# Two passes of 256 token columns instead of one pass of 512 in the matrix multiplications of a hybrid encoder trunk

## The reference, cut to what matters

```python
def swiglu(x, w_gate, w_up, w_down):
    return (jax.nn.silu(x @ w_gate) * (x @ w_up)) @ w_down

def hybrid_mixer(u, w_in, ...):
    proj = u @ w_in
    qa, ka, va, us, qc, kc, vc, fc = jnp.split(proj, IN_SPLITS, axis=-1)
    ya = swa_sink_attention(qa, ka, va, ...)     # sliding window
    yb = s5_mixer(us, ...)                       # state space scan
    yc = fox_attention(qc, kc, vc, fc, ...)      # forgetting attention
    y = jnp.concatenate([rms_norm(ya, ga), rms_norm(yb, gb), rms_norm(yc, gc)], axis=-1)
    return y @ w_out

for l in range(DEPTH):                           # DEPTH = 2
    h = h + 0.5 * rms_norm(swiglu(rms_norm(h, g[0]), ffn1_gate[l], ffn1_up[l], ffn1_down[l]), g[1])
    h = h + rms_norm(hybrid_mixer(rms_norm(h, g[2]), w_in[l], ..., w_out[l], cos, sin), g[3])
    h = h + 0.5 * rms_norm(swiglu(rms_norm(h, g[4]), ffn2_gate[l], ffn2_up[l], ffn2_down[l]), g[5])
```

## Time and profile before

| | us |
|---|---|
| median of the two runs | 2172.43 |
| the two runs | 2170.24 and 2174.62 |
| span of the profiled execution, first to last instruction | 2170.5 |
| PE busy in it | 2018.1 (93%) |
| DVE busy | 1206.8 (56%) |
| ACT busy | 875.6 (40%) |

### The profile page before, as it was taken

How to read it: one execution, slowest core, us unless ns; L and a number is a source line. 1 busy time by engine, 2 the same in 40 slices (tenths; PEclk the granted TensorE clock), 3 DMA queues, 4 the chain that set the end, 5 groups by cost and what they waited for, 6 DMA issues and landing times.

```text
span 2170.5 us, 27124 instructions
## 1 busy us (share of the span) xinstructions
PE 2018.1 (93%) x8694; PEld 1553.9 (72%) x8694; DVE 1206.8 (56%) x1645; ACT 875.6 (40%) x1380; POOL 436.5 (20%) x609
## 2 busy tenths in 40 slices
PE   5999999897998999999979999998889989999996
PEld 4888878564556688888758888885545667888885
DVE  3666643479864655553255555236887655555423
ACT  4444422343453544442144444224334635444322
POOL 4666765435400000000000000004552000000000
PEclk8999999999999999999989999999989999999998
DMA  4444344232102233333213333323210123333320
GB/s 113 121 126 121 116 129 125 77 88 69 39 20 69 68 97 97 97 113 93 66 58 99 97 96 105 107 69 98 78 59 20 40 59 88 96 96 100 116 84 39
DMA packets 330105, 187.03 MB, mean 86 GB/s; under 512 B 6440, under 2 KB 324304, under 8 KB 330032
## 3 DMA queue, kind: packets, MB, share of 16 engines
q1 hardware_dynamic: 323696, 167.08, 26.6%
q0 software_dynamic: 6336, 19.05, 2.8%
HBM read 175.59 MB, written 10.49 MB: 86 GB/s over the span
## 4 chain that ended last, share of the span: by engine, by line
PE 75%; DVE 11%; issue 7%; ACT 5%; DVEq 0%; POOL 0%; DMA 0%; SPq 0%; ACTq 0%; POOLq 0%
PE ps L375 16%; PE ps L377 15%; PE ps L376 15%; PE ps L451 7%; PE ps L452 7%; PE ps L453 7%; PE ps L413 2%; DVE rot L1289 1%; DVE wl L1089 1%; PE ps L528 1%; ACT wh L712 1%; PE ps L596 1%; DVE prob L1340 1%; PE ps L516 1%; DVE gst L1302 1%
## 5 line engine op out<-in xcount | busy, mean ns | idle before, releaser
L375 PE MATMUL ps<-xh,wh 128*128 128x512 f32 x1776 | 714.6, 402 | 66.3 <-DVE xl L1099 48.2
L376 PE MATMUL ps<-xl,wh 128*128 128x512 f32 x1776 | 697.7, 393 | 0.0
L377 PE MATMUL ps<-xh,wl 128*128 128x512 f32 x1776 | 697.5, 393 | 0.0
L1089 DVE TENSOR_TENSOR wl<-raw,wh 128x1024 fp32r<-128x1024 f32 (+1 forms) x288 | 387.0, 1344 | 527.0 <-ACT wh L712 523.2
L712 ACT ACTIVATE wh<-raw 128x1024 fp32r<-128x1024 f32 (+1 forms) x288 | 322.1, 1119 | 461.6 <-PE ps L453 317.7
L375 PEld LDWEIGHTS ps<-xh,wh 128*128 128x128 f32 x1776 | 336.9, 190 | 182.9 <-DVE wl L1089 45.6
L377 PEld LDWEIGHTS ps<-xh,wl 128*128 128x128 f32 x1776 | 337.1, 190 | 72.3
L376 PEld LDWEIGHTS ps<-xl,wh 128*128 128x128 f32 x1776 | 337.8, 190 | 69.6 <-issue 3.1
L451 PE MATMUL ps<-Hh,wh 128*128 128x512 f32 x704 | 276.5, 393 | 2.5 <-DVE wl L1089 2.4
L452 PE MATMUL ps<-Hl,wh 128*128 128x512 f32 x704 | 277.2, 394 | 0.0
L453 PE MATMUL ps<-Hh,wl 128*128 128x512 f32 x704 | 273.4, 388 | 0.0
(11 more groups left out here) (208 smaller groups left out, 2009.6 us busy)
## 6 DMA issues: line engine op xcount, KB each, us to landing
raw<-in_ffn_gate SPq DMA_DIRECT2D x88, 512.0 KB, 3.7
raw<-in_ffn_up SPq DMA_DIRECT2D x88, 512.0 KB, 3.8
raw<-in_ffn_down SPq DMA_DIRECT2D x64, 704.0 KB, 4.4
raw<-in_w_in SPq DMA_DIRECT2D x28, 512.0 KB, 3.8
ssm_tables<-tabw POOLq DMA_DIRECT2D x32, 256.0 KB, 2.5
tab<-ssm_tables POOLq DMA_DIRECT2D x16, 512.0 KB, 3.7
raw<-in_w_out SPq DMA_DIRECT2D x16, 512.0 KB, 3.8
yF<-in_x SPq DMA_DIRECT2D x1, 2048.0 KB, 9.5
```

The costliest lines, as they stand in the source:

```text
L375: pe.matmul(bank, wh[:, slot, kw, :], xh[:, kx, :], start=first, stop=False)
L376: pe.matmul(bank, wh[:, slot, kw, :], xl[:, kx, :], start=False, stop=False)
L377: return pe.matmul(bank, wl[:, slot, kw, :], xh[:, kx, :], start=False, stop=last)
L1089: V.tensor_tensor(wl[:, slot2, 0:nk, :], raw[:, slot4, 0:nk, :], wh[:, slot2, 0:nk, :].bitcast(F32), ALU.subtract).then_inc(w_split, 1)
```

## The change

`unit_x` no longer calls `three` but a new helper `three_of`, which takes a slice of the tokens. It goes through the unit's 8 blocks for tokens 0 to 255, and then again for tokens 256 to 511. `first_two`, `project_half` and the down projection keep their 512 columns. The matmul that clears the marks of the bank is still only the first one of the unit; the two halves write different columns of the bank. Waits and signals are where they were: one wait on `w_split` ahead of the unit, and one increment of `unit_done` behind it.

```diff
+            def three_of(out_, slot, kw, kx, tok, first, last):
+
+                pe.matmul(out_, wh[:, slot, kw, :], xh[:, kx, tok], start=first, stop=False, skip_group_check=True)
+                pe.matmul(out_, wh[:, slot, kw, :], xl[:, kx, tok], start=False, stop=False, skip_group_check=True)
+                return pe.matmul(out_, wl[:, slot, kw, :], xh[:, kx, tok], start=False, stop=last, skip_group_check=True)
+
             def unit_x(n, slot, bank, k0=0, nk=KD):
 
                 pe.wait_ge(w_split, n + RAW_SLOTS + 1)
-                for k in range(nk):
-                    mm = three(bank, slot, k, k0 + k, k0 + k == 0, k0 + k == KD - 1)
+                for half in range(2):
+                    tok = slice(half * (SEQ // 2), (half + 1) * (SEQ // 2))
+                    for k in range(nk):
+                        mm = three_of(bank[:, tok], slot, k, k0 + k, tok, half == 0 and k0 + k == 0, k0 + k == KD - 1)
                 mm.then_inc(unit_done, 1)
```

## The result

The changed kernel takes 2228.97 us (two runs, 2228.85 and 2229.09) against 2172.43 us, a ratio of 1.026 with an interval of 1.0241 to 1.028: 56.5 us slower. The profiled execution is the run of 2228.85 us, its span 2227.3 us.

A forecast was written before the change was run, and what follows sets the result against it. TensorE's matmul starts were taken to bound the changed loops; 4656 × 2.3 ns = 10.7 us, with loads free, took the span from 2170.5 to 2181.2, plus 1.9 to the median: 2183 us, range 2158 to 2240.

The forecast's parts named there:

- What bounds the kernel: In the gate and up loop, how often TensorE can start a matmul sets the end; one every 226 ns.
- How many: In `unit_x`, 4656 of 8694 matmuls become 9312 of 256 columns, adding 4656 weight loads and 4656 starts.
- The weight loads: In the cut units, 256 columns hide a full weight load, only 2.3 ns stay fixed; the loads cost nothing.
- The third rival: In the cut units, fp32r loads can't run under 256 columns: +220 ns a pair, +1026 us, 3199 us; chance 0.04.
- rival 2: In the cut units, the extra time disappears for narrow streams: 109 ns each, −40 us, 2132 us; chance 0.07.
- rival 4: In the cut units, 256-column fp32r streams run at fp32's rate: +205 ns a pair, +955 us, 3127 us; chance 0.05.
- The other 11 ns: In `unit_x` matmuls, 11.1 ns go with the columns: 114.5 ns per half, +2.3 ns a pair, +10.7 us.
- rival 1: At every start in `unit_x`, 11.1 ns are paid once per matmul or load: +63 us, 2235 us; chance 0.30.
- The range: For the whole kernel, 2158 to 2240 us, to hold 8 in 10, reaching up to the fixed price.
- the forecast's own range: For the whole kernel, 2160 to 2206 us, from 112 to 117 ns per 256-column matmul; chance 0.54.
- The signs named for a fixed price: In the gate and up loop, starts 120 ns apart and a 256-column fp32r record 282 ns long.
- The chain of VectorE and ScalarE: In the gate and up loop, 10.4 us hidden under 10.9 us of PE, 0.5 us to spare in two units.

The follow-up runs named there:

- shift 24: Bursts added behind the end of the kernel before, streamed columns shifted by 24 numbers against the weights: 233.3 ns at 512 columns, 119.9 at 256.
- shift 48: Bursts added behind the end of the kernel before, streamed columns shifted by 48 numbers against the weights: 233.3 ns at 512 columns, 113.3 at 256.
- the alternating bursts: Bursts behind the end of the kernel before, alternating 128 and 64 weight columns: 117 ns each; alternating fp32r and bfloat16 at 256 columns: 245 ns a pair.
- the new place: Changed kernel with unused tiles of 64 bytes ahead of `wh` and 192 ahead of `Hh`: 2167.44 us; kernel before with both: 2195.55 us.
- the third bursts: Bursts behind the end of the kernel before, streaming `Hh`, `Hl` or shifted columns and weights: `Hh` 229 and 117.8 ns, shifted `xl` 116.7 to 120.

## Why the prediction was wrong

- **What bounds the kernel** was right. The halves start every 120 ns in all of the loop, and what they cost more went to the end, less 6 us of waits.
- **How many**: 4656 were counted and came, and the down projection kept its pace.
- **The weight loads** were right: 256 columns hide a full load. The third rival falls with the timeline: 120 ns from start to start and a load of 190 ns under way in each. The rule that the Trainium skill has for it ("TensorE: Matmul & The Clock Gate", "Part 3: Packing small matmuls — row/col tiling"), that loads overlap only with another row group, doesn't hold in this kernel by the same rows; the same section also lets a load of the background weight buffer go ahead, which no run here tells apart. There is indeed no slack beyond: a load takes 111 ns (bursts of 192 and 128 columns). The third digit of the 109 ns came from transposes, whose loads last 0.14 us and not 0.19, so rival 2's 109 ns was not to be had in a chain of full fp32r loads; the least that any run shows for 256 fp32r columns is 113.3.
- **The type's rate** does not fall at 256 columns (rival 4): the record is 283 ns, columns at one per cycle and the same rest as before.
- **The step that failed is "The other 11 ns"**, where the 11.1 ns were read as going with the columns. A half costs 120.0 ns and not 114.5, so the term 4656 × 2.3 = 10.7 us is 4656 × 13.3 = 61.9 us. That is the price of rival 1, the fixed one. Neither piece of evidence carried the reading. The records of 394 and 388 ns are not a matter of the operands: a burst of `Hh` alone has 388, 392 and 394 in turn. What the rows did hold was that a whole down matmul takes 229 ns against 226.7, which is the place of the tile. And that the extra vanishes at half clock says nothing between the readings: halves start every 213.3 ns there, with nothing left over, though at full clock their price is the fixed one. The text called it no proof and took it as evidence all the same.
- **The range** holds 2229 us only because its upper end was stretched to the fixed price, which had a chance of 0.30; the forecast's own range ended at 2206. The signs named for a fixed price came as written, 120 ns between starts and a record of 283 ns where 282 was given. That the kernel turns slower by 2% once "more than 9 of the 11.1 ns are fixed" is a slip: with the rest going with the columns, 109 + 11.1/2 + f/2 = 118 gives f = 7.
- **Rival 1's sum** of 2235 us was 6 us too high, since it left out the waits that a slower PE covers: 6.0 us by the rows. The prediction left those out as being small, which beside +10.7 us they were not.
- **Rival 1's mechanism** is only half of it. Over the width the price is constant at this place (13.3 ns at 512, 384, 320 and 256 columns). But it isn't a price of a start or of a load as such: bfloat16 with the same starts and loads pays 2.5 ns. At shift 24 a whole pays 20 and a half 13; at shift 48, 20 and 6.6, a half less than half as much: there the change gains. Which of my readings is nearer, and with it the sign of the change, depends on an offset within 256 bytes that neither the diff nor the profile shows, and on which of two patterns a stage falls into.
- **"The chain of VectorE and ScalarE"** was to have 0.5 us to spare and more with a slower PE: waits for `wl` fell from 4.3 + 2.4 to 1.8 + 0.5 us.
- **Left open**: how the hardware comes to this. Reads for a stream and for a load that meet in SBUF would fit that the price depends on the type's bytes, on the weight columns and on places, but this is a guess that no run shows, and the two simple forms of it, a price by the own load or by the next, failed in the alternating bursts, and narrower weights make 512 columns slower. Nor is it known why one place holds two prices in one run, 113.4 and 117.8 in the gate and up stages at the new place, 118.0 and 113.8 in the down projections in halves. Steady patterns into which a sequence falls, the rival to the places in the expectation of the third bursts, are so not excluded beside them.

## What to carry to other kernels

When a matmul takes longer than its columns, measure the distance between starts at both widths before cutting or joining it, in a burst behind the kernel's end: what one width shows can't be divided into a fixed and a proportional part. For fp32r measure also at some offsets of weights and columns to each other within 256 bytes, since this one parameter moved the same cut from +2.6% to some −1%, and an unused tile of 192 bytes brought 227 ns in place of 229 in the down projection. Do not cut below the time of a load: 256 columns hid it; 128 did not, and took 111 ns where they are 53 ns of a whole matmul. Above it, what a cut cost was the price of a start, 2.5 ns in bfloat16 and 13.3 ns in fp32r at this place.

## What the runs showed of the hardware that was not expected

- fp32r costs 226.7 to 234.7 ns at 512 columns and 113.3 to 120 ns at 256, in part by the relative place of weights and columns in SBUF; the least of either is 226.7 ns for 512 columns. At the kernel's place bfloat16 costs 215.8 and 109.2; fp32, in two passes, 429.2 and 215.8 in a burst.
- In the traces the distances within a burst settle, after some 8 matmuls, into a pattern that repeats; one place can have two (113.4 and 117.8 ns), each held for a stage of nearly 2000 matmuls.
- 64 weight columns in place of 128 make 256 columns faster (120 to 113.3) and 512 slower (226.7 to 230).
- At half clock 256 fp32r columns start every 213.3 ns, columns alone: the 13.3 ns are gone.
- A load of 128 fp32r columns bounds the distance at 111 ns; with 32 weight columns 128 columns start every 60 ns. In bfloat16 128 columns with a load of 128 columns each start every 56 ns; that load's record is 0.10 us long, the fp32r one's 0.19.
